# First layer on unscaled rows, blocks cleared together, and the state space's output table at other half pieces

## The reference

```python
h = rms_norm(x, even_norm_g[i])            # x * rsqrt(mean(x*x) + EPS) * g, a factor per token
proj = h @ even_w_in[i]                    # 1024 x 5120
q, k, v, z_a, u, z_b = jnp.split(proj, ...)  # 1024, 1024, 1024, 1024, 512, 512 columns
q = rms_norm(q.reshape(bsz, L, SB_HEADS, SB_HEAD_DIM), sb_q_norm_g[i])
k = rms_norm(k.reshape(bsz, L, SB_HEADS, SB_HEAD_DIM), sb_k_norm_g[i])
o_a = stick_breaking_attention(q, k, v) * jax.nn.silu(z_a)
o_b = s5_mixer(u, ...) * jax.nn.silu(z_b)  # y = Re(C h) + d*u, gelu, then a gated product (glu)
x = x + jnp.concatenate([o_a, o_b], axis=-1) @ even_w_out[i]
```

## Time and profile before

| | us |
|---|---|
| median of 3 runs | 1024.98 |
| lowest and highest run | 1024.74, 1026.59 |
| profiled execution, its own time | 1024.8 |
| its span in the trace | 1023.0 |
| PE busy in it | 994.5 (97%) |
| DVE busy | 731.1 (71%) |
| ACT busy | 571.5 (56%) |
| POOL busy | 212.2 (21%) |

### The profile page before, as it was taken

The page is one execution under the profiler, slowest core; times in us unless marked ns, Lnnn a source line. Parts: engine busy times, 40 slices in busy tenths (PEclk is TensorE's granted clock), DMA queues, the critical chain, the costliest instruction groups (busy, mean ns, idle before and its releaser), DMA issues.

```text
span 1023.0 us, 13858 instructions
## 1 busy us (share of the span) xinstructions
PE 994.5 (97%) x5308; PEld 848.2 (83%) x5308; DVE 731.1 (71%) x1178; ACT 571.5 (56%) x894; POOL 212.2 (21%) x204
## 2 busy tenths in 40 slices
PE   6999999999999999999999999999999999999996
PEld 5778889888988788888888888868888888888884
DVE  7984945978769768777777585674766547768666
ACT  6759568657456555555554355555545545434453
POOL 5800070000000014432235000010664001620001
PEclk9999999999999999999999999999999999999998
DMA  7633433768747488875656455636776345644551
GB/s 269 187 125 100 133 122 111 255 214 284 230 132 244 129 312 316 303 243 185 206 169 191 135 158 185 202 118 203 247 247 218 122 146 184 185 144 147 184 183 42
DMA packets 56242, 192.07 MB, mean 188 GB/s; under 512 B 8576, under 2 KB 8832, under 8 KB 56176
## 3 DMA queue, kind: packets, MB, share of 16 engines
q1 hardware_dynamic: 52592, 180.35, 54.7%
q0 software_dynamic: 3152, 10.36, 3.0%
q10 hardware_dynamic: 432, 0.49, 0.1%
HBM read 189.59 MB, written 1.05 MB: 186 GB/s over the span
## 4 chain that ended last, share of the span: by engine, by line
PE 89%; DVE 8%; ACT 1%; issue 1%; DMA 0%; POOL 0%; DVEq 0%; ACTq 0%
PE G L672 15%; PE G L674 15%; PE G L673 15%; PE G L698 15%; PE G L700 7%; DVE WL L1713 2%; PE B L632 2%; PE B L1028 1%; PE G L728 1%; PE G L730 1%; PE G L729 1%; PE G L681 1%; PE G L683 1%; PE G L684 1%; PE B L1008 1%
## 5 line engine op out<-in xcount | busy, mean ns | idle before, releaser
L1713 DVE TENSOR_TENSOR WL<-RAW,WH 128x1024 fp32r<-128x1024 f32 (+2 forms) x294 | 364.9, 1242 | 189.9 <-ACT WH L1161 189.1
L1161 ACT ACTIVATE WH<-RAW 128x1024 fp32r<-128x1024 f32 (+2 forms) x294 | 308.5, 1050 | 214.7 <-PE G L674 137.1
L672 PE MATMUL G<-WH,HT 128*128 128x512 f32 (+2 forms) x556 | 224.9, 404 | 5.1 <-DVE WL L1713 4.4
L698 PE MATMUL G<-HT,WH 128*128 128x512 f32 x640 | 226.9, 399 | 0.0
L674 PE MATMUL G<-WL,HT 128*128 128x512 f32 (+2 forms) x556 | 215.2, 387 | 0.0
L673 PE MATMUL G<-WH,HT 128*128 128x512 f32 (+2 forms) x556 | 214.3, 385 | 0.0
L700 PE MATMUL G<-HT,WL 128*128 128x256 f32 x640 | 179.4, 280 | 0.0
L698 PEld LDWEIGHTS G<-HT,WH 128*128 128x128 f32 x640 | 120.2, 188 | 29.7 <-issue 0.5
L672 PEld LDWEIGHTS G<-WH,HT 128*128 128x128 f32 x556 | 105.2, 189 | 26.7 <-DVE WL L1713 5.0
L674 PEld LDWEIGHTS G<-WL,HT 128*128 128x128 f32 x556 | 104.8, 189 | 21.4
L700 PEld LDWEIGHTS G<-HT,WL 128*128 128x128 f32 x640 | 120.8, 189 | 0.6 <-issue 0.5
(11 more groups left out here) (369 smaller groups left out, 1479.8 us busy)
## 6 DMA issues: line engine op xcount, KB each, us to landing
RAW<-in_w_in SPq DMA_DIRECT2D x176, 512.0 KB, 3.6
RAW<-in_even_w_in SPq DMA_DIRECT2D x40, 512.0 KB, 3.6
AR<-in_w_ada_t SPq DMA_DIRECT2D x32, 512.0 KB, 4.7
RAW<-in_odd_w_in SPq DMA_DIRECT2D x16, 512.0 KB, 4.5
AR<-in_w_ada_g POOLq DMA_DIRECT2D x32, 256.0 KB, 3.9
RAW<-in_w_proj_ret SPq DMA_DIRECT2D x16, 512.0 KB, 3.5
RAW<-in_w_out SPq DMA_DIRECT2D x16, 512.0 KB, 3.6
RAW<-in_even_w_out SPq DMA_DIRECT2D x12, 512.0 KB, 3.8
```

The lines of the kernel that those rows point to most:

```text
L672: nc.tensor.matmul(o, xh, wh, start=begins, stop=False)
L698: nc.tensor.matmul(o[:, :], wh[:, c], flat(HT[:, k, :, :]), start=k == 0, stop=False, skip_group_check=True)
L1161: return nc.scalar.activation(out_, ps, ACT.Copy, **kw)
L1713: vt(wl, raw, wh.bitcast(F32), ALU.subtract).then_inc(*dve.mark(LO, n))
```

## The change

**Unscaled rows.** Layer 0 now turns X itself (`UNSCALED = (0, 1)`), and the factor NR comes in where results leave PSUM: ACT's Square and copy of heads and v get `scale=NR`, za's Tanh gets HR (half of NR), and `sb_gate` multiplies by HR. For the turned groups u and zb the factor varies along the free side. So DVE makes two diagonals RD = identity times NR, PE multiplies ones by RD (`factor_row`, after half 4), ACT copies the row to RB, and DVE, no longer ACT, takes u out with a product by RB (events U_V); zb leaves by a DVE product into ZS (ZB_V), ACT's Tanh on ZS and DVE's silu. Both rstd are one pass over two columns. HN, its DVE and POOL steps and their events are gone.

**Front order.** ACT first loads its table, then issues CI, then cols, and waits for cols; its copies of tile 0, `hi(0)`, those of tile 1, `hi(1)`, `hi(2)` now stand ahead of the squares. DVE's row follows this. SP loads RAW's piece 0 between the two tiles of X. **Blocks cleared at once.** POOL's clears stand first, without a wait; its DMAs (BR first) wait for `hi(0)`.

**Output table.** `out_re` and `out_im` go from halves 18 and 21 to 38 and 40, ACT's packing from 25 and 28 to 48 and 50, with other blocks of memory for the intermediates (halves of SZA, and CB). **Dots.** The last four stand at halves 146, 149, 151, 153, not 146, 150, 154, 158. ACT's table for silu is loaded at half 147, ahead of its use.

```diff
@@ tables @@
-AT_S5 = {... "in_re": 12, "in_im": 15, "out_re": 18, "out_im": 21,
+AT_S5 = {... "in_re": 12, "in_im": 15, "out_re": 38, "out_im": 40,
-         "block": {2: "b0", 18: "cp", 19: "hre", 22: "him", 25: "re", 28: "im"}, ...
+         "block": {2: "b0", 18: "cp", 19: "hre", 22: "him", 48: "re", 50: "im"}, ...
-AT_DOT0 = (82, 86, 90, 94, 98, 116, 118, 120) + tuple(130 + 4 * i for i in range(8))
+AT_DOT0 = (82, 86, 90, 94, 98, 116, 118, 120, 130, 134, 138, 142, 146, 149, 151, 153)
+AT_ROW = 4
-UNSCALED = (1,)
+UNSCALED = (0, 1)
@@ blocks @@
-        CD = flat(KT[:, 0:2, :]).rearrange("p (r i k) -> p r i k", r=2, i=16)
+        CD = YFh[:, 2048:2560].rearrange("p (r i k) -> p r i k", r=2, i=16)
-        OA_, OB_, OC_ = QT1, KT1, flat(VB1)
+        OA_, OB_, OC_ = flat(SZA)[:, 0:1024], flat(SZA)[:, 1024:2048], CB[:, :]
@@ PE @@
+            def factor_row():
+                ps = take(("rb",), R_A.of("row"))
+                pe.wait_ge(*R_V.of("diagonal"))
+                nc.tensor.matmul(ps[:, 0:256], ONES, RD, start=True, stop=True).then_inc(*told("rb"))
@@ s5_out, PE: waits for the packed table @@
+                pe.wait_ge(*S5_BLOCK.of("im"))
@@ head_sums, ACT @@
+                act.wait_ge(*ROWS.of(0))
                     ...
-                    copy(TK[:, i % 2, ti, :], gbank(name, ti)[:, :]).then_inc(...)
+                    copy(TK[:, i % 2, ti, :], gbank(name, ti)[:, :], scale=NR[0][:, ti:ti + 1]).then_inc(...)
@@ evac0, ACT @@
-                        silu_half(name, SZB[:, ti, :], gbank(name, ti)[:, :], ti)
+                        act.wait_ge(*ZB_V.of(ti))
+                        nc.scalar.activation(SZB[:, ti, :], ZS[:, ti, :], ACT.Tanh, scale=0.5).then_inc(*act.mark(TH, name, ti))
@@ front, ACT @@
+            nc.scalar.preload_act_table_set("natural_log_exp_and_others")
+            nc.scalar.dma_start(CI[:, :], t["consts"][:, 0:256]).then_inc(l_ci, 16)
             nc.scalar.dma_start(PC, t["cols"]).then_inc(l_cols, 16)
-            nc.scalar.dma_start(CI[:, :], t["consts"][:, 0:256]).then_inc(l_ci, 16)
@@ ACT, half 147 @@
+                if time == AT_GLA["states"][2]:
+                    nc.scalar.preload_act_table_set("silu_and_others")
@@ evac0, DVE @@
+                    if name in ("u", "zb"):
+                        dve.wait_ge(*tile(name, ti))
+                        dve.wait_ge(*R_A.of("row"))
+                    if name == "u":
+                        vt(UT[:, 2 * ti:2 * ti + 2, :].rearrange("p j (t c) -> p j c t", t=4),
+                           pair(gbank(name, ti)).rearrange("p j (c t) -> p j c t", t=4),
+                           RB.rearrange("p (c t) -> p c t", t=4).unsqueeze(1).to_broadcast([P, 2, 64, 4]),
+                           ALU.mult).then_inc(*dve.mark(U_V, ti))
                     ...
-                        silu(name, SZB[:, ti, :], gbank(name, ti)[:, :], ti)
+                        vt(ZS[:, ti, :].rearrange("p (a b) -> p a b", a=2), pair(gbank(name, ti)),
+                           RB.unsqueeze(1).to_broadcast([P, 2, 256]), ALU.mult).then_inc(*dve.mark(ZB_V, ti))
+                        silu(name, SZB[:, ti, :], ZS[:, ti, :], ti)
@@ POOL @@
-            nc.gpsimd.dma_start(BR, t["s5_b"]).then_inc(l_br, 16)
-            for ti in range(2):
-                scaled(0, ti)
-            pool.wait_ge(*HN_V.of(0, 1))
             for r in range(2):
                 nc.gpsimd.memset(H[r].rearrange("p a b -> p (a b)"), 0.0).then_inc(*pool.tick())
             ...
+            pool.wait_ge(*HI.of(0))
+            nc.gpsimd.dma_start(BR, t["s5_b"]).then_inc(l_br, 16)
@@ SP @@
-            for ti in range(2):
-                nc.sync.dma_start(X[:, ti, :], xv[:, ti, :]).then_inc(l_x[ti], 16)
+            nc.sync.dma_start(X[:, 0, :], xv[:, 0, :]).then_inc(l_x[0], 16)
             load(0)
+            nc.sync.dma_start(X[:, 1, :], xv[:, 1, :]).then_inc(l_x[1], 16)
```

More of the change, by code:

```diff
@@ L91 @@
 TURNED, FOLDED = ("u", "zb", "glu", "gk", "gq"), ("qa", "ka", "qr", "kr")
-AT_S5 = {"powers": 1, "cos": 3, "lp": 4, "factor": 7, "c": 9, "in_re": 12, "in_im": 15, "out_re": 18, "out_im": 21,
+AT_S5 = {"powers": 1, "cos": 3, "lp": 4, "factor": 7, "c": 9, "in_re": 12, "in_im": 15, "out_re": 38, "out_im": 40,
          "heads": (24, 49), "table": {23: 0, 26: 1, 27: 2, 28: 3, 29: 4, 30: 5},
-         "block": {2: "b0", 18: "cp", 19: "hre", 22: "him", 25: "re", 28: "im"}, "near": (27, 28, 29, 30),
+         "block": {2: "b0", 18: "cp", 19: "hre", 22: "him", 48: "re", 50: "im"}, "near": (27, 28, 29, 30),
          "near_out": (32, 34), "turn": (35, 37, 38, 39), "in": (40, 42, 45, 47), "scan": (52, 54),
@@ L158, in program @@
         TK = sb("TK", [P, 2, 2, 512])
+        RB = sb("RB", [P, 256])[:, :]
         CI = sb("CI", [P, 256])
@@ L496, in program @@
         L2, H4 = range(2), range(4)
-        ROWS = events("rows", [1])
+        ROWS = events("rows", [0, 1])
         SUMSQ = events("sumsq", [(0, 0), (0, 1)] + [(l, ti, n) for l in range(1, 5) for ti in L2 for n in L2])
[L500 to L504, removed]
+        RSTD = events("rstd", [(l, ti) for l in range(5) for ti in L2 if l > 1 or ti])
+        HN_V, HN_A = (events(f"hn_{e}", [(l, ti) for l in (2, 3) for ti in L2]) for e in "va")
+        R_V, R_A = events("r_v", ["diagonal"]), events("r_a", ["row"])
+        TURNS = ([(0, ti, r) for ti in L2 for r in H4]
                  + [(1, ti, 2 * q + r) for q in L2 for ti in L2 for r in L2]
@@ L1080, in tensor_program @@
                 half(time)
+                if time == AT_ROW:
+                    factor_row()
                 if time in AT_TURN1:
@@ L1302, in head_sums @@
                     act.wait_ge(*squared[ti])
-                    copy(TK[:, i % 2, ti, :], gbank(name, ti)[:, :]).then_inc(*act.mark(HEAD_SQ, name, ti))
+                    copy(TK[:, i % 2, ti, :], gbank(name, ti)[:, :], scale=NR[0][:, ti:ti + 1]).then_inc(*act.mark(HEAD_SQ, name, ti))
             def evac0(name):
@@ L1555, in scalar_program @@
                     evac0(ENDS[time])
+                if time == AT_ROW:
+                    act.wait_ge(*side("rb"))
+                    copy(RB, bank_of["rb",][:, 0:256]).then_inc(*act.mark(R_A, "row"))
                 if time == 1:
@@ L2369, in vector_program @@
             nc.vector.memset(M3[:, :, :, :].rearrange("p a b c -> p (a b c)"), 0.0).then_inc(*dve.mark(S5_V, "zero"))
-            for ti in range(2):
-                rstd(0, ti)
-                scaled(0, ti)
+            for r in range(4):
+                turned(0, 0, r)
             lo(0)
-            for q in range(2):
-                for ti in range(2):
-                    for r in range(2):
-                        turned(0, ti, 2 * q + r)
-                lo(1 + q)
+            for r in range(4):
+                turned(0, 1, r)
+            lo(1)
+            lo(2)
+            rstd(0, slice(0, 2))
+            rows(0)
             ts(gqs, co["sb_q_g"], 128.0 ** -0.5, None, ALU.mult).then_inc(*dve.mark(GQS, "q"))
```

64 lines of the change are left out of this document (31 added, 33 removed).

## The result

The changed kernel took 1031.8 us (median of 4 runs, 1030.55 to 1032.85) beside 1024.91 before: ratio 1.0054, 95% interval 1.0029 to 1.0079. It is slower, by 0.5%, and the interval leaves out 1; the forecast was 1026.4 and its range ended at 1029.0. The profiled execution took 1032.85, span 1031.0, 8.0 us more than the span of before.

A forecast was written before the change was run, and what follows sets the result against it. PE was taken as the bound, busy 994.5 of 1023.0 us. Terms -1.1 (to half 40), +1.6 (46), +1.9 (84), -0.9 (dot) gave +1.45: 1026.25 profiled, 1026.4 us median; eight-in-ten range 1023.2 to 1029.0.

The forecast's parts named there:

- The front: Start to half 6: first product near 12.3, ACT's first copy at 7.0, half 6 at 24.0; +0.45 us.
- Both ends of my range: ACT's first copy of HT: early end 6.35 us, late end 8.6, both from CI's landing plus four transposes.
- The wait at half 6: PE waits for lo(3) at half 6, about 1.5 us; 1 to 2 us was a sign of being right.
- the rival with the late identity: Table load holds the issue, first copy at 8.6, u at ACT's strided price: +3.45, 1028.4 us; chance 0.25.
- u: Two DVE products with strided result ahead of lo(6): 1.6 us, between 1.2 and 2.1, all reaching PE.
- +2.6: Delay of half 20, near 46.3 instead of 43.72: 0.45 front, 1.6 u, 0.5 delayed small angle steps.
- The output table: Moving out_re and out_im removes waits at halves 24 and 26, 3.7 us; out_re hidden at 38; -1.1 to half 40.
- The wait at 46: out_im at half 40 not hidden, so PE waits for lo(23) at half 46: +1.6 us.
- My walk to 106.57: DVE's steps from 98.58 through lo(23) end at 106.57, where half 46 had started at 104.98.
- zb: DVE product, ACT tanh, DVE silu per half: chain of 3.9 us, making PE wait at half 84, +1.9.
- what I had granted the waits at 24 and 26: Each wait costs PE 0.15 to 0.2 us more than its listed figure; 0.35 for both.
- The dot: Last dot goes to half 153, in idle time, so the 0.9 us wait on YTl goes: -0.9.

The follow-up runs named there:

- mended: Changed kernel with out_im at half 39, GpSimd's two large steps after in_im, zb's two DVE products ahead of its silus: 1025.77 us.
- pool_later: Changed kernel, but GpSimd makes DD and the decay block only once DVE has finished in_im: 1031.11 us.
- table_back: Changed kernel with the output table's steps back at halves 18 and 21, packing at 25 and 28, old blocks: 1030.1 us.
- table_only: Kernel before with the output table's move alone (halves 38 and 40, packing 48 and 50, new blocks): 1023.84 us.
- heads_unscaled: Changed kernel without the factor at the heads' Square and copy, so q and k lack it: 1030.62 us.
- dots_only: Kernel before with the last dots' new places and the early silu table load alone: 1023.7 us.
- wait_46: Kernel before with table steps at halves 38, 39, changed dots and table load, three unread DVE products between lo(22) and lo(23): 1022.97 us.
- wait_46_long: Kernel before with table steps at halves 38, 39, changed dots and table load, five unread DVE products between lo(22) and lo(23): 1026.58 us.

## Why the prediction was wrong, step by step

**The front** held by its numbers: first copy 7.20 (7.0), first product 12.33 (12.3), half 6 at 23.55 (24.0), and the start's gain was gone there. The first copy was partly luck. Both ends of my range reckon from CI's landing and four transposes. CI landed at 5.60, which gives 6.75 by that sum; what held the copy was cols, which took 6.0 us from its issue and not 4.3. The wait at half 6 was 0.58, not the 1 to 2 us named as a sign: lo(3) was 0.45 earlier than forecast. Of the rival with the late identity the identity did not come, since the table load did not hold the issues; its strided price for u did.

**u** was mis-sized: 2.03 us for two against my 1.6. That is ACT's strided price and not DVE's plain one: the same product by RB with a plain result, for zb, takes 0.68 for one and 1.28 for two (mended). The sentence from the Trainium skill, "SBUF — State Buffer", section "Specifications (TRN2)", had pointed to that end, and this trace agrees with it. The two errors cancel, which is luck: the front brought 0.45 less than forecast and u 0.43 more, so at half 14 the sum stood at +2.6, what I had forecast for half 20. pool_later, without the collision that comes next, reached half 20 at 46.17 (forecast 46.3).

**The collision moved** (1.5 us, the first real miss). My sum has no term for GpSimd's two large steps at all. I read L2042's 1.96 us as the table's own, though a step of the same shape takes 1.23 (L2048), and did not see that GpSimd's steps of 46.23 and 48.15 lay beside it and beside lo(12) (2.05 us). In the changed kernel they begin 3.6 us earlier, at 42.59, and in_im comes 2.6 us later, at 42.27. So they met in_im, on the path to lo(10): half 20 at 47.86, not 46.3. pool_later shows it. The table's move is not the cause: table_back has the steps back and the same in_im of 2.69 + 1.68 us. The Trainium skill, "SBUF — State Buffer", section "Who interferes with whom", says that a DVE instruction with two inputs in SBUF contends with a GpSimd instruction that reads SBUF; the 1.68 against 0.96 us of the same step is this case's number for it.

**The output table**: the gain against before, 3.8 against 3.7, and out_re hidden, as forecast. On the kernel before the move alone brings those 3.8 (table_only). In the changed kernel I credited the table with more than was its own: with its steps back PE waited 0.48 us there, about 2.2 without the 1.7 at half clock ahead of it (an estimate), because the collision no longer lay on out_re. The gain at 24 and 26 and the loss at 20 are in part one thing, counted in two places. The wait at 46 came, but 2.5 us with its part at 44, not 1.6, because my sum has no term for the factor in the heads' Square and copy: eight Squares at 0.09 more and two longer copies, 0.9 us on ACT ahead of hi(22) (heads_unscaled). My walk to 106.57 adds up to 106.52, which changes nothing.

**zb**: the chain ran 4.07 us by the trace (3.9), the wait cost 2.2 (1.9).

```profile
191.14 0.68 DVE L1962 TENSOR_TENSOR AR<-G,RB 128x512 f32<-128x512 f32 x1
192.53 0.69 DVE L1894 SCALAR_TENSOR_TENSOR AR<-AR 128x512 f32<-128x512 f32 x1 [0.70 <-ACT AR L1330]
193.13 0.68 DVE L1962 TENSOR_TENSOR AR<-G,RB 128x512 f32<-128x512 f32 x1
194.52 0.69 DVE L1894 SCALAR_TENSOR_TENSOR AR<-AR 128x512 f32<-128x512 f32 x1 [0.70 <-ACT AR L1330]
```

```profile
197.44 0.36 PE L686 MATMUL B<-YTh,WH 128*128 128x256 f32 x1 [2.04 <-DVE YTl L2145]
```

Half of the difference is the longer chain; the other half is what I had granted the waits at 24 and 26 and forgot here: a listed wait costs PE 0.15 to 0.2 more than its figure (2.04 listed, 2.20 between the starts). Another 0.3 came in small delays at halves 85 to 94; that a DVE late behind zb makes them is likely and not shown.

**The dot** brought 1.1, its 0.9 with the same addition. Another 0.2 at half 160 is not its work (dots_only).

**Not in the sum**: w_gate's DMA, which landed 5.7 us after its issue instead of 5.0, 0.75 us. In other runs of this family PE waited 0 to 0.8 us for it; I did not settle why.

**The clock** (3.4 us in the profiled run, the largest miss). No step of mine had a price for PE running at half clock, though I forecast new waits of 1.5 to 2 us at half pieces 6, 12, 46 and 84 and summed only their length. Without the two stretches the profiled time would be 1029.4: still above my range, by 0.4. The lowest run, 1030.55 at a mean clock of 0.996, lies above it too. So the steps above alone would have failed it as well.

The sum of the misses: collision 1.5, heads 0.9, zb and behind it 0.6, w_gate 0.75, less 0.4 at halves 160 and 164 and small differences, is 3.1 above the 1.45; the clock adds 3.4: 8.0.

What stays open is why a stretch comes in one run and not in the next, and why so often between 58 and 68 us, where PE is fully busy, but much of it with small matmuls (L831 reads 32 partitions, L837 has 32 columns). The table's move alone, with fewer waits than before, had it in 6 of 9 runs; I made no run that changes these small matmuls.

## What to carry to other kernels

A change that shifts two engines by different amounts makes other steps meet: for each large GpSimd step with SBUF inputs write down which DVE step lies beside it before and after. A factor put "for free" into a ScalarE instruction has a price per instruction; look for a row with and without it. And a new wait of TensorE of 1.5 us or more is not priced by its length alone: put beside it a chance that the clock falls, here 1.7 us a time. How large the chance is differed: with waits of 1.76 and 1.57 us the kernel before had a clock of 0.995 or less in 8 of 33 runs, wait_46 with one of 1.6 us in 7 of 12. The output table's move, with its second step one half piece earlier and without the unscaled rows, gained 5.5 us together with the dots; one half piece later, it brings PE a new wait.

## What the runs showed of the hardware that I had not expected

- The granted clock fell inside a 4.2 us wait of PE and stayed at the 1.2 GHz level for nearly 6 us of full work behind it (wait_46_long). The Trainium skill, "TensorE: Matmul & The Clock Gate", section "Part 1: The HAM clock gate", says that the gate follows how busy PE has recently been. This run agrees; the half clock from 59 to 72 us in the profiled run of wait_46, with PE counted busy throughout, is not explained by what I can read in its rows.
- The kernel before has the effect too: in the last group 23 of 33 runs lie under 1025.8, and eight at 1026.3 and more have a mean clock of 0.995 or less. The two left, at 1026.16 and 1026.20, have 0.998: something else lengthened them.
- ACT's Square of 128x128 from PSUM with a factor per row starts every 0.34 us instead of 0.25 (a whole row of eight, changed kernel and heads_unscaled).
- DVE's product from PSUM with a result strided by 256 bytes takes 1.0 us for 512 elements a row, plain 0.6.
- Two DMA issues went out beside the ACT table load (0.78 and 1.20 inside 0.74 to 2.02).
